# Sliding-window attention in a two-layer encoder: from blocks of 128 queries to chunks of 64

## The reference, cut to what matters

```python
def sink_attention(q, k, v, sinks, mask):
    s = jnp.einsum('...lhgd,...mhd->...hglm', q, k).astype(jnp.float32) * (HEAD_DIM ** -0.5)
    if mask is not None:
        s = jnp.where(mask, s, NEG)
    sink = jnp.broadcast_to(sinks.astype(jnp.float32)[..., None, None], s.shape[:-1] + (1,))
    p = jax.nn.softmax(jnp.concatenate([s, sink], axis=-1), axis=-1)[..., :-1]
    return jnp.einsum('...hglm,...mhd->...lhgd', p.astype(v.dtype), v)
...
    a = swa_prompt(q_a, k_a, v_a, sinks)      # 8 heads of 64, 2 KV heads, chunks of 64, 2 chunks back
...
    merged = jnp.concatenate([rms_norm(a, p['norm_a']), rms_norm(b, p['norm_b']), c], axis=-1) @ p['w_out']
```

## Time and profile before

| what | value |
|---|---|
| median of 3 runs | 1435.47 us (1434.57 to 1435.71) |
| the profiled execution, its own time | 1433.33 us |
| its span | 1431.4 us |
| TensorE busy (PE) | 1374.2 us, 96% of the span |
| VectorE busy (DVE) | 688.7 us, 48% |
| ScalarE busy (ACT) | 505.5 us, 35% |
| GpSimd busy (POOL) | 214.2 us, 15% |
| mean granted TensorE clock | 0.985 of full |

### The profile page before, as it was taken

One profiled execution on the slowest core, in us unless ns is written; L12 is line 12 of the kernel. 1 busy time (PEld: TensorE's weight loads), 2 busy tenths in 40 slices (PEclk: granted clock), 3 DMA queues, 4 the chain that ended last, 5 costly groups with the idle time before them and its releaser, 6 DMA issues.

```text
span 1431.4 us, 24272 instructions
## 1 busy us (share of the span) xinstructions
PE 1374.2 (96%) x10358; PEld 1321.3 (92%) x10358; DVE 688.7 (48%) x1320; ACT 505.5 (35%) x1088; POOL 214.2 (15%) x257
## 2 busy tenths in 40 slices
PE   8999888999999999999999998799999999999996
PEld 7889857999999999999998897599999999999996
DVE  6645783465444444211467477817544444441213
ACT  4222375544322223222433235736522322232220
POOL 6411201520000000011343021124100000001110
PEclk9999999999999999999999999999999999999998
DMA  4411200212222222222222120002222222222211
GB/s 161 162 45 63 67 1 1 90 60 103 89 75 89 82 81 89 75 89 88 75 104 89 47 84 30 1 30 89 89 79 84 89 75 89 77 87 89 74 60 66
DMA packets 33643, 107.96 MB, mean 75 GB/s; under 512 B 4304, under 2 KB 8928, under 8 KB 33536
## 3 DMA queue, kind: packets, MB, share of 16 engines
q1 hardware_dynamic: 31056, 101.26, 20.5%
q0 software_dynamic: 2480, 5.15, 1.1%
HBM read 103.25 MB, written 3.15 MB: 74 GB/s over the span
## 4 chain that ended last, share of the span: by engine, by line
PE 81%; DVE 12%; issue 2%; ACT 2%; POOL 0%; POOLq 0%; DVEq 0%; ACTq 0%
PE psum L449 25%; PE psum L451 25%; PE psum L450 25%; DVE h_lo L1233 1%; DVE mx L1481 1%; PE psum L546 1%; DVE x L1281 1%; PE psum L469 1%; DVE prob L1496 1%; DVE rsq L1368 1%; PE psum L744 1%; PE psum L459 1%; ACT prob L882 1%; PE psum L570 1%; DVE h_whole L1509 1%
## 5 line engine op out<-in xcount | busy, mean ns | idle before, releaser
L449 PE MATMUL psum<-h_hi,w_hi 128*128 128x320 f32 (+1 forms) x2192 | 660.6, 301 | 4.2 <-DVE hid_whole L1270 2.5
L450 PE MATMUL psum<-h_lo,w_hi 128*128 128x320 f32 (+1 forms) x2192 | 650.6, 297 | 0.0
L451 PE MATMUL psum<-h_hi,w_lo 128*128 128x320 f32 (+1 forms) x2192 | 650.6, 297 | 0.0
L449 PEld LDWEIGHTS psum<-h_hi,w_hi 128*128 128x128 f32 x2192 | 417.2, 190 | 10.2 <-issue 3.2
L450 PEld LDWEIGHTS psum<-h_lo,w_hi 128*128 128x128 f32 x2192 | 417.2, 190 | 2.8 <-issue 2.5
L451 PEld LDWEIGHTS psum<-h_hi,w_lo 128*128 128x128 f32 x2192 | 417.1, 190 | 0.0
L1226 DVE TENSOR_TENSOR w_lo<-raw,w_hi 128x1024 fp32r<-128x1024 f32 x184 | 232.9, 1272 | 320.5 <-ACT w_hi L882 320.4
L882 ACT ACTIVATE w_hi<-raw 128x1024 fp32r<-128x1024 f32 x184 | 192.5, 1050 | 178.3 <-DMA raw<-in_wts 178.1
L449 PE MATMUL psum<-hid_hi,w_hi 128*128 128x256 f32 (+1 forms) x672 | 198.1, 295 | 0.0
L451 PE MATMUL psum<-hid_hi,w_lo 128*128 128x256 f32 (+1 forms) x672 | 197.7, 294 | 0.0
L450 PE MATMUL psum<-hid_lo,w_hi 128*128 128x256 f32 (+1 forms) x672 | 197.7, 294 | 0.0
(11 more groups left out here) (173 smaller groups left out, 1226.3 us busy)
## 6 DMA issues: line engine op xcount, KB each, us to landing
raw<-in_wts SPq DMA_DIRECT2D x184, 512.0 KB, 3.2
tab<-in_tabs POOLq DMA_DIRECT2D x2, 642.0 KB, 5.1
x<-in_xT SPq DMA_DIRECT2D x2, 640.0 KB, 10.4
lp<-in_lpar POOLq DMA_DIRECT2D x2, 640.0 KB, 5.7
out_x<-x SPq DMA_DIRECT2D x4, 320.0 KB, 2.3
tab<-in_tabs POOLq DMA_DIRECT2D x2, 577.0 KB, 4.5
x<-in_xT SPq DMA_DIRECT2D x2, 512.0 KB, 5.8
out_x<-x SPq DMA_DIRECT2D x4, 256.0 KB, 2.1
```

Source lines behind the costliest of these rows:

```text
L449: pe.matmul(out, wh, hi, start=first, stop=False)
L450: pe.matmul(out, wh, lo, start=False, stop=False)
L451: return pe.matmul(out, wl, hi, start=False, stop=last)
```

## The change

A unit is now a chunk c of 64 queries with all eight heads: the two heads of a pair lie in the two halves of the partitions, the four pairs beside each other in the free dimension. Keys are the 192 that the chunk sees (64 for chunk 0, 128 for chunk 1), so no mask is laid. One maximum goes over four times 192 columns in two banks, one tensor-by-tensor multiplication normalises all four pairs, the turned probabilities come in a part of 128 keys (bank 4, copied by ScalarE) and a part of 64 (bank 5, copied by VectorE), and a values matmul has 64 columns of v as weights under 4 x 64 = 256 columns. v is kept in two alignments (seven tiles of 128 and one of 64), so there are eight transposes of it, and they move into the input projection. The loop's depth is one chunk for the turn, two for the values. The output projection of the first six tiles is cut in two: k = 4 to 7 (b and c) first, k = 0 to 3 (a) later.

```diff
-CYCLE = (0, 2, 6, 7, 1, 3)
+CYCLE = (2, 3, 0, 1, 7, 6)
 NORM_BANK = (4, 5)
-SUM_AT = 400
-K_OUT = (4, 5, 6, 7, 0, 1, 2, 3)
+SUM_AT = 320
...
+CHUNKS = T // CHUNK
+KEYS0 = [0, 0] + [CHUNK * (c - 2) for c in range(2, CHUNKS - 1)] + [SEQ]
+WINDOW = [(P, CHUNK), (0, P)] + [(0, P + CHUNK)] * (CHUNKS - 2)
+KW = P + CHUNK
+V_CACHE, V_NEW, VTILES = 8, 9, 10
+VTILE = [(None, 0), (0, None)] + [(c // 2 - 1, c // 2) if c % 2 == 0 else (4 + (c - 3) // 2, 4 + (c - 1) // 2)
+                                  for c in range(2, CHUNKS - 1)] + [(V_CACHE, V_NEW)]
...
+SPLIT_AT = 3
+MERGED = [(g, k) for ks in (range(4, KT), range(4)) for g in (0, 1) for k in ks]
+EARLY = KT
...
+                    for i in range(4):
+                        pe.transpose(banks[4][:, i * P:(i + 1) * P], vv[:, i * P:(i + 1) * P], ident[:, :])
+                    for i in range(3):
+                        t0 = CHUNK + i * P
+                        pe.transpose(banks[5][:, i * P:(i + 1) * P], vv[:, t0:t0 + P], ident[:, :])
+                    pe.transpose(banks[5][0:CHUNK, 3 * P:4 * P], vv[:, SEQ - CHUNK:SEQ], ident[:, :])\
+                      .then_inc(vk_done, 1)
+                def v_new():
+                    pe.wait_ge(rstd_kept, L(KEPT["b"] + 2, KEPTS))
+                    pe.transpose(banks[6][0:DEC, 0:P], vv[:, SEQ:T], ident[:, :]).then_inc(vk_done, 1)
...
+                fill[16].append(v_tokens)
...
+                def scores(c):
+                    o, n = WINDOW[c]
+                    if c == 0:
                         pe.wait_ge(dve_took, L(2 * IN_T, V_TOOK))
                         pe.wait_ge(cache_landed, L(1, 1) * CACHES * 16)
+                    elif c >= 2:
+                        pe.wait_ge(p_ready, L(c - 1, CHUNKS))
+                    for j in range(4):
+                        for h in (0, 1):
+                            at = (j % 2) * KW + o
+                            mm = pe.matmul(banks[2 * (c % 2) + j // 2][64 * h:64 * h + 64, at:at + n],
+                                           qq[:, j, c * CHUNK:(c + 1) * CHUNK], kk[:, h, KEYS0[c]:KEYS0[c] + n],
+                                           start=True, stop=True, tile_position=(0, 64 * h))
                     mm.then_inc(s_done, 1)
+                def turn(c):
+                    wide, half = VTILE[c]
+                    if c == 0:
+                        pe.wait_ge(vk_ready, L(1, 2))
+                    else:
+                        pe.wait_ge(pt_ready, L(WIDE[c - 1], WIDE[-1]))
+                        pe.wait_ge(half_ready, L(HALF[c - 1], HALF[-1]))
+                    pe.wait_ge(pn_ready, L(c + 1, CHUNKS))
+                    for j in range(4):
+                        if wide is not None:
+                            mm = pe.transpose(banks[4][:, j * P:(j + 1) * P], prob[:, c % 2, j, 0:P], ident[:, :])
+                        if half is not None:
+                            mm = pe.transpose(banks[5][0:CHUNK, j * P:(j + 1) * P], prob[:, c % 2, j, P:KW],
+                                              ident[:, :])
+                    mm.then_inc(pt_done, 1)
+                def values(c):
+                    wide, half = VTILE[c]
+                    b, at = c // 2, c % 2 * CHUNK
+                    if c == 0:
+                        pe.wait_ge(ro_taken, L(NB, NB))
+                        pe.wait_ge(state_ready, L(NB, NB))
                         pe.wait_ge(vk_ready, L(2, 2))
+                    elif c >= 4 and c % 2 == 0:
+                        pe.wait_ge(a_taken, L(b - 1, NB))
+                    pe.wait_ge(pt_ready, L(WIDE[c], WIDE[-1]))
+                    pe.wait_ge(half_ready, L(HALF[c], HALF[-1]))
+                    parts = [(t, src, n) for t, src, n in ((wide, wideT, P), (half, halfT, CHUNK)) if t is not None]
+                    for h in (0, 1):
+                        out = banks[6 + b % 2][64 * h:64 * h + 64, :].rearrange("p (j n) -> p j n", n=P)
+                        for i, (t, src, n) in enumerate(parts):
+                            probs = src[0:n, c % 2, :].rearrange("p (j h q) -> p j h q", h=2, q=CHUNK)
+                            mm = pe.matmul(out[:, :, at:at + CHUNK], vk[0:n, t, 64 * h:64 * h + 64], probs[:, :, h, :],
+                                           start=i == 0, stop=i == len(parts) - 1, tile_position=(0, 64 * h))
                     mm.then_inc(o_done, 1)
...
+                def part_out(i, ks, ready):
+                    m, g = OUT_ORDER[i]
+                    pe.wait_ge(lo_made, L(S_OUT + m + 1, SLOTS))
+                    pe.wait_ge(h_ready, L(HR["merged"] + ready, HRS))
+                    for k in ks:
+                        mm = three(dense(i, g), L(S_OUT + m, SLOTS), k, h_hi[g][:, k, :], h_lo[g][:, k, :],
+                                   k == 4, k == 3)
+                    if 3 in ks:
+                        mm.then_inc(tile_done, 1)
+                bc, a_ = range(4, KT), range(4)
+                for c in range(CHUNKS + 2):
+                    if c < CHUNKS:
+                        scores(c)
+                    if c == 0:
+                        v_new()
+                    if 1 <= c < CHUNKS + 1:
+                        turn(c - 1)
+                    if c == CHUNKS + 1:
+                        part_out(0, bc, 4)
+                    if c >= 2:
+                        values(c - 2)
+                part_out(1, bc, 4)
+                pe.wait_ge(pt_ready, L(WIDE[-1], WIDE[-1]))
+                pe.wait_ge(half_ready, L(HALF[-1], HALF[-1]))
+                sum_tokens(l, "a", 0, acc, 4, [(a_ssq, L(2, NB))])
+                pe.wait_ge(p_ready, L(CHUNKS, CHUNKS))
+                part_out(2, bc, 4)
+                spread(l, "a", 0, 4)
+                part_out(3, bc, 4)
+                sum_tokens(l, "a", 1, acc, 5, [(a_ssq, L(NB, NB))])
+                pe.wait_ge(a_taken, L(NB, NB))
+                part_out(4, bc, 8)
+                spread(l, "a", 1, 5)
+                part_out(5, bc, 8)
+                for i in range(4):
+                    part_out(i, a_, 12)
+                part_out(4, a_, 16)
+                part_out(5, a_, 16)
...
+                    fn(vk[:, 0:4, :], tiles(banks[4]), ACT.Copy)
+                    fn(vk[:, 4:7, :], tiles(banks[5][:, 0:3 * P]), ACT.Copy)
+                    fn(vk[0:CHUNK, 7, :], banks[5][0:CHUNK, 3 * P:4 * P], ACT.Copy).then_inc(vk_ready, 1)
...
+                more[17].append(vk_copy)
...
+                def exps(c):
+                    o, n = WINDOW[c]
+                    act.wait_ge(nm_ready, L(c + 1, CHUNKS))
+                    if c >= 2:
+                        act.wait_ge(pt_done, L(c - 1, CHUNKS))
+                    for j in range(4):
+                        fn(prob[:, c % 2, j, o:o + n], score_at(c)[:, j // 2, j % 2, :], ACT.Exp,
+                           bias=nm[:, c % 2, j:j + 1], scale=SCALE, accum_out=den[:, c % 2, j:j + 1])
+                    fn(es[:, c % 2, :], sm[:, c % 2, :], ACT.Exp).then_inc(p_ready, 1)
+                def turned(c):
+                    if VTILE[c][0] is None:
+                        return
+                    act.wait_ge(pt_done, L(c + 1, CHUNKS))
+                    if c >= 2:
+                        act.wait_ge(o_done, L(c - 1, CHUNKS))
+                    fn(wideT[:, c % 2, :], banks[4], ACT.Copy).then_inc(pt_ready, 1)
...
+                for c in range(CHUNKS + 2):
+                    if c < CHUNKS:
+                        exps(c)
+                    if c == 0:
+                        vk_new()
+                    if c == CHUNKS:
+                        preload(ACT.Sqrt)
+                    if c == SPLIT_AT:
                         split(L(S_IN + IN_T - 1 + RING, SLOTS))
+                    if 1 <= c < CHUNKS + 1:
+                        turned(c - 1)
+                    if c >= 3 and c % 2:
+                        outs((c - 3) // 2)
+                    if 1 <= c <= EARLY:
+                        hi_of_merged(c - 1)
+                outs(NB - 1)
+                root(l, "a", 0, 4, SWA_HEADS * HD)
+                keep(l, "a", 0, acc, 4)
+                root(l, "a", 1, 5, SWA_HEADS * HD)
+                for n in range(EARLY, EARLY + 4):
+                    hi_of_merged(n)
+                keep(l, "a", 1, acc, 5)
+                for n in range(EARLY + 4, len(MERGED)):
                     hi_of_merged(n)
...
+                def maxima(c):
+                    dve.wait_ge(s_done, L(c + 1, CHUNKS))
+                    ns = nsink[:, l, :]
+                    if c >= 2:
+                        dve.wait_ge(p_ready, L(c - 1, CHUNKS))
+                    link(dve.tensor_reduce(mx[:, c % 2, :].rearrange("p (b j) -> p b j", b=2), score_at(c), AX.X, ALU.max))
+                    link(dve.scalar_tensor_tensor(out=nm[:, c % 2, :], in0=mx[:, c % 2, :], scalar=-SCALE,
                                                   in1=ns, op0=ALU.mult, op1=ALU.min))
```

(39 more changed lines are left out.)

## The result

The changed kernel takes 1480.97 us (median of four runs, 1476.30 to 1482.93) against 1435.02 us of the kernel before measured beside it: ratio 1.0316, 95% interval 1.0291 to 1.0340, slower by 46 us. The forecast was 1461 us and slower, the range 1429 to 1482. Lines of the code have moved: the dense products stand at L460 to L462, scores at L714, turn at L729 and L731, values at L751; on VectorE the maximum is L1484, the half copy L1496, the normalising L1504 and L1505.

A forecast was written before the change was run, and what follows sets the result against it. The serial attention chain through TensorE and VectorE was taken as the bound; 0.3 (stages) + 1.8 (transposes) + 24 (clock falls) = 26.1 on 1433.33 us gave 1459.4, median forecast 1461; own range 1446 to 1478, wide range 1429 to 1482.

The forecast's parts named there:

- the third rival: Scores of full chunks go in single file, 1.25 us more in seven chunks; total time 1479 to 1500 us; chance 0.11.
- The signs named beforehand: Full chunks: scores 7.5 to 11 us apart, TensorE idle about 3.3, reduce near 0.95, multiplication near 0.98, values near 2.0.
- scores near 2.7: Sign of a wrong forecast: a full chunk's scores on TensorE take near 2.7 us, meaning mispriced shapes; 1.45 was taken.
- stages at full clock less those of before: Attention stages of both layers: 83.4 us each, 1.2 less than layer 0, 1.5 more than layer 1, in all +0.3.
- transposes of v in the input projection: Eight transposes moved ahead of the last input tile, uncovered there: 0.9 us a layer, +1.8 in all.
- falls of the clock: Clock falls behind TensorE's waits in the attention loop: 12 us a layer, 24 in all, bounds +7 to +48.
- five of seven, 2.4 each: Of seven TensorE waits a layer in the chunk loop, five are followed by a clock fall costing 2.4 us each.
- 2.7 + 16.5: Each layer's stage: 2.7 us from first scores to first maximum, then 16.5 until chunk 4's scores are done.
- The upper bound of 2.3: Values of a full chunk on TensorE: bounds 1.0 (paired) and 2.3 us, with 2.0 taken.
- the row taken: Last block's eight 64-column records alternating the same two shapes, 1.03 us; from it values were priced at 2.0 us.
- The clock holds: Rival for the attention loop: at most a few short clock falls; 1436 to 1443 us, point 1438; chance 0.15.
- The values run in pairs: Rival at values(c): both array halves overlap, seven chunks give back 1.0 each, 14 us; 1424 at full clock; chance 0.21.

The follow-up runs named there:

- the run at full clock: Changed kernel with eleven 128x128 matmuls of ones added in front of every turn but the last: 1439.88 us, ratio 1.0036 to the kernel before.
- two runs: Changed kernel with eleven added matmuls before every turn but the last, 1439.88 us; the same plus each chunk's values ordered by parts, 1423.80 us.

## Why the prediction was right, and where it was off

**The mechanism was right.** The loop is serial through VectorE, TensorE waits about 3.3 us in each full chunk, the clock falls behind the waits, and this makes the kernel slower. Undoing either link shows it: the version with work in the waits is 41 us shorter, the one with VectorE's order exchanged 54.

**The number came out with luck.** The median of 1480.97 us is 20 us above the point of 1461, outside the forecast's own range (1446 to 1478) and 1 us inside the wide one, which reached so far because of the third rival. It even lies among that rival's times, 1479 to 1500, though its condition, scores in single file, did not hold: they took 1.52 us at full clock. The signs named beforehand are mixed for the same reason: scores of full chunks stand 10.4 to 11.7 us apart (7.5 to 11 was named), and "scores near 2.7", which was to mean mispriced shapes, is there as 2.83 us, but at half clock.

**The sum, term by term**, against the 42.8 us by which the profiled span grew:

| term | forecast, us | measured, us |
|---|---|---|
| stages at full clock less those of before | +0.3 | 2 x 86.4 - 84.6 - 81.9 = +6.3 |
| transposes of v in the input projection | +1.8 | 2 x 0.86 = +1.7 |
| falls of the clock | +24 (+7 to +48) | 16.2 + 18.4 = +34.6 |
| sum | +26.1 | +42.6 |

The first and the third row share out the 40.9 us of the stages, and the run with the added matmuls draws the line between them.

**The falls were too few, not too cheap.** "I take five of seven, 2.4 each": it was eight waits a layer, all followed by a fall. The wait at the first turn, 3.97 us, was missing from the count. Sparing two in seven was a guess: among the waits of the earlier trace rows, 2.41 us had no fall and 2.50 had one, and the new waits lay above both. Yet length alone does not decide. The earlier trace rows left out a wait in front of the attention, behind which the clock of the kernel before stayed at 1.00; the same wait in the changed kernel was followed by 0.50:

```profile
28.34 0.68 PE L469 MATMUL psum<-ident,rec 128*128 128x128 f32 x4 [3.12 <-DVE rec L1246]
...
28.69 1.19 PE L480 MATMUL psum<-ident,rec 128*128 128x128 f32 x4 [3.13 <-DVE rec L1253]
```

Why all sixteen waits of the new loop were followed by a fall, and some others of 3.1 us were not, the runs do not show. Per wait the price was 16.2 / 8 = 2.0 us in layer 0 and 18.4 / 8 = 2.3 in layer 1, near the 2.4 taken. The remark that TensorE's part is on the chain in the new loop was what carried this price: the fall behind the eighth turn of the kernel before cost nothing, so the reading of the earlier trace rows as 3.4 us lost would have been wrong there.

**The serial chain was 3 us a layer too short.** In the run at full clock chunk 4's scores are done 19.4 us behind the first scores, against 2.7 + 16.5 = 19.2. Four full chunks took 33.2 us, against 31.2, and the rest 33.8 against 33.0. A chunk there is 3.49 us from the end of the scores to the turn (3.35), 1.46 + 1.02 for scores and turn (2.45) and 2.29 for the values (2.0): 8.26 us. So the values are the largest mis-sized term, 0.29 of 0.46 us a chunk, and the wait is 0.14. The upper bound of 2.3 was right; the row taken, eight records of the last block in the earlier trace rows, was read as a cost of alternation for short matmuls that longer ones would hide, and the halves simply did not overlap.

**VectorE's and TensorE's other prices hold.** Maximum 0.96 us (0.95), normalising 0.96 (0.98), half copy 0.68 (0.68), scores 1.52 in pairs (1.45). The rows of the changed kernel for v, on TensorE:

```profile
162.32 1.18 PE L470 MATMUL psum<-ones,gv 128*128 128x1 f32 x10
163.43 0.65 PE L634 MATMUL psum<-ident,vv 128*128 128x128 f32 x4
...
164.28 0.36 PE L460 MATMUL psum<-h_hi,w_hi 128*128 128x256 f32 x1
```

From the sums over tokens to the next dense product it is 1.96 us; in the kernel before the same two starts are 161.62 and 162.72, 1.10 us apart. The difference is 0.86, forecast 0.9; ScalarE's copies cost nothing, as its wait there is still 5.50 us (the earlier trace rows had 5.67).

**The rivals.** Neither "The clock holds" nor "The values run in pairs" came true in the change; two runs made their conditions. The saving by values in pairs was right: 14 us was forecast, and at full clock it is 2 x 7.2. The totals, 1439.88 us for 1436 to 1443 and 1423.80 for 1424, fit in part by luck. The stages at full clock were 6 us dearer in all than priced, but in both profiled executions the clock stayed at 1.00 behind the waits ahead of the attention, where the kernel before lost time (0.50 from 66 to 70 us). The scores went in pairs, not in single file.

## What to carry to other kernels

When a pipeline is made shallower, write down for each engine's queue what stands ahead of the piece that the other engine waits for: a short copy behind an operation that needs the newest data makes the whole loop serial, and reversing their order undoes it. On a serial loop count every wait of TensorE of about 3 us (2.8 to 4.0 here) as a likely fall of its clock and price it on TensorE's share of the chain; where other engines set the pace, a fall can be free, and where TensorE is busy throughout it is paid. Put matmuls of one tile shape next to each other, both column halves before the next shape.

## What was not expected

Useless work made a run shorter: with 43.5 us of matmuls put into waits the two stages lost 34.6 us. A change of loop order on TensorE alone, with waits of the same length (3.43 against 3.38 us), came with a clock over the stage of 0.68 instead of 0.82 and 0.77. The same wait, in the same code, was followed by a fall of the clock in one execution and not in another (3.12 and 3.13 us). And two halves of the array that ran side by side in 0.58 us when neighbours needed 1.15 when a part with other rows stood between them.
